# Bias and row maximum in one VectorE instruction, on negated logits, in two attention stages

## The reference

```python
q = rms_norm((h @ w_q).reshape(B, T, H, 2, d), q_norm)
s = jnp.einsum('bhcqd,bhckd->bhcqk', qb, k_sh) * scale          # scale = 64 ** -0.5 = 0.125
bias = -slopes[:, None, None] * dist                            # slopes = 2 ** -(h + 1)
s = jnp.where(dist >= 0, s + bias[None, :, None], -jnp.inf)
p = jax.nn.softmax(s, axis=-1)
attn = p[:, :, 0] - lam_full * p[:, :, 1]
o = jnp.einsum('bhqk,bhkd->bhqd', attn, v_sh)
```

```python
s_win = einsum(qr, k_win) * scale + bias
s_ctx = einsum(qr, kc) * scale
p = jax.nn.softmax(jnp.concatenate([s_win, s_ctx], axis=-1), axis=-1)
o = einsum(p_win, v_win) + einsum(p_ctx, vc)
```

## Time and profile before

| | |
|---|---|
| median of 3 runs | 3286.02 us (3283.83 to 3288.11) |
| the profiled execution | 3282.35 us |
| its span, first to last instruction | 3280.6 us |
| PE / DVE / ACT / POOL busy | 3061.7 / 1621.9 / 1126.9 / 134.8 us |
| mean granted TensorE clock | 0.962 |
| bytes moved | 234.75 MB, mean 72 GB/s |

### The profile page before, as it was taken

The page is one execution under the profiler, slowest core; times in us unless marked ns, Lnnn a source line. Parts: engine busy times, 40 slices in busy tenths (PEclk is TensorE's granted clock), DMA queues, the critical chain, the costliest instruction groups (busy, mean ns, idle before and its releaser), DMA issues.

```text
span 3280.6 us, 38579 instructions
## 1 busy us (share of the span) xinstructions
PE 3061.7 (93%) x15565; PEld 2389.7 (73%) x15565; DVE 1621.9 (49%) x2633; ACT 1126.9 (34%) x1821; POOL 134.8 (4%) x145
## 2 busy tenths in 40 slices
PE   7999898999999799999999999769999988987998
PEld 6888754666667688888788888547888865776886
DVE  5434454555555554344744345775435445336335
ACT  4322224444444333223332234453323243324332
POOL 0000001111211100000000000000000000101000
PEclk9999898999999899999999999879999988998999
DMA  4333212111110133333233332003333210201331
GB/s 125 96 99 97 83 61 67 41 41 41 42 29 21 44 105 97 97 97 92 82 97 98 99 98 95 1 1 103 98 95 92 80 54 1 78 23 52 94 90 58
DMA packets 186182, 234.75 MB, mean 72 GB/s; under 512 B 14201, under 2 KB 127446, under 8 KB 185750
## 3 DMA queue, kind: packets, MB, share of 16 engines
q1 hardware_dynamic: 186006, 232.29, 23.0%
HBM read 228.05 MB, written 4.19 MB: 71 GB/s over the span
## 4 chain that ended last, share of the span: by engine, by line
PE 86%; DVE 8%; ACT 3%; issue 2%; POOL 1%; DMA 0%; SPq 0%; DVEq 0%; ACTq 0%
PE banks L871 62%; PE banks L996 3%; PE banks L1028 2%; PE banks L982 1%; PE banks L1378 1%; PE banks L1369 1%; PE banks L1363 1%; PE banks L1019 1%; PE banks L1063 1%; PE banks L1092 1%; PE banks L1088 1%; PE banks L960 1%; DVE diff_scores L2391 1%; DVE diff_small L2397 1%; PE banks L1037 1%
## 5 line engine op out<-in xcount | busy, mean ns | idle before, releaser
L1935 DVE TENSOR_TENSOR weights_lo<-weights_raw,weights_hi 128x1024 fp32r<-128x1024 f32 (+3 forms) x377 | 453.4, 1206 | 996.9 <-ACT weights_hi L1454 996.3
L871 PE MATMUL banks<-operand_hi,weights_hi 128*128 128x512 f32 x2080 | 822.9, 396 | 34.8 <-DVE weights_lo L1935 13.1
L871 PE MATMUL banks<-operand_lo,weights_hi 128*128 128x512 f32 x2080 | 816.4, 392 | 0.0
L871 PE MATMUL banks<-operand_hi,weights_lo 128*128 128x512 f32 x2080 | 816.0, 392 | 0.0
L1454 ACT ACTIVATE weights_hi<-weights_raw 128x1024 fp32r<-128x1024 f32 (+3 forms) x377 | 391.9, 1043 | 1055.3 <-PE banks L871 1028.4
L871 PEld LDWEIGHTS banks<-operand_hi,weights_hi 128*128 128x128 f32 x2080 | 394.3, 190 | 125.7 <-issue 28.2
L871 PEld LDWEIGHTS banks<-operand_lo,weights_hi 128*128 128x128 f32 x2080 | 394.6, 190 | 83.2 <-issue 2.2
L871 PEld LDWEIGHTS banks<-operand_hi,weights_lo 128*128 128x128 f32 x2080 | 394.2, 190 | 83.5
L871 PE MATMUL banks<-hidden_ffn_hi,weights_hi 128*128 128x512 f32 x352 | 137.1, 390 | 0.0
L871 PE MATMUL banks<-hidden_ffn_lo,weights_hi 128*128 128x512 f32 x352 | 136.9, 389 | 0.0
L871 PE MATMUL banks<-hidden_ffn_hi,weights_lo 128*128 128x512 f32 x352 | 136.9, 389 | 0.0
(11 more groups left out here) (522 smaller groups left out, 4406.8 us busy)
## 6 DMA issues: line engine op xcount, KB each, us to landing
weights_raw<-in_ffn_w_in_dram SPq DMA_DIRECT2D x352, 256.0 KB, 3.2
weights_raw<-in_ffn_w_out_dram SPq DMA_DIRECT2D x88, 512.0 KB, 3.8
weights_raw<-in_w_in_dram SPq DMA_DIRECT2D x36, 512.0 KB, 3.7
weights_raw<-in_rwkv_w_rkv_dram SPq DMA_DIRECT2D x24, 512.0 KB, 4.3
weights_raw<-in_w_mod_dram SPq DMA_DIRECT2D x24, 512.0 KB, 5.5
weights_raw<-in_w_kv_dram SPq DMA_DIRECT2D x16, 512.0 KB, 3.7
weights_raw<-in_rwkv_w_o_dram SPq DMA_DIRECT2D x8, 512.0 KB, 5.6
weights_raw<-in_diff_w_q_dram SPq DMA_DIRECT2D x8, 512.0 KB, 4.9
```

Source lines behind the costliest of these rows:

```text
L871: mm = nc.tensor.matmul(o, l, r, start=first and t == 0 and job["opens"], stop=last and t == 2, **skip)
L1935: nc.vector.tensor_tensor(ring_lo[0:p, u["slot"], 0:n, 0:w], ring_raw[0:p, u["ring"], 0:n, 0:w], f32(ring_hi[0:p, u["slot"], 0:n, 0:w]), A ...
```

## The change

Logits are kept negated, so that the row's maximum becomes a minimum and can be used as the exponential's bias without a further step. One VectorE instruction, `tensor_tensor_reduce`, adds two tensors, multiplies by a constant, writes the result and also gives the minimum of the row (started from a scalar).

In the differential attention the slope of the head is divided out of the queries (`q_gain`, eight columns made at the start of the query stage), so that scores and distance can be added without a factor; the new instruction multiplies the sum by -0.125 times the slope. Maximum and negation of step 1 go, and ScalarE waits for step 0. In the neighbourhood attention the context keys are negated when they are copied; VectorE first reduces the minimum of the 256 context scores, then the new instruction adds the bias to the 512 window scores, negates, and continues that minimum. This all stands in step 0, lane by lane.

```diff
+            for h_ in range(DIFF_HEADS):
+                nc.vector.tensor_scalar(q_gain[:, h_:h_ + 1], vec("diff_q_norm"), 1.0 / slope(h_), None,
+                                        ALU.mult).then_inc(*dve_own.by())
...
-                        head_scale("q", ui - 1, q[:, ui - 1], vec("diff_q_norm"))
+                        if ui == 1:
+                            dve.wait_ge(*dve_own.now())
+                        head_scale("q", ui - 1, q[:, ui - 1], q_gain[:, ui - 1:ui])
...
                 if tb < TB and s == 0:
                     for c, b in ((0, A), (1, B)):
                         dve.wait_ge(*lane_pe[lane].at(("s", h_, tb, c)))
-                        nc.vector.scalar_tensor_tensor(
-                            out=S[:, lane, c, 0:n], in0=dist[:, (TB - 1 - tb) * P:T], scalar=8.0 * 2.0 ** (-(h_ + 1)),
-                            in1=ps[:, b, 0:n], op0=ALU.mult, op1=ALU.add).then_inc(*own.by(("bias", h_, tb, c)))
-                elif tb < TB and s == 1:
-                    for c in range(2):
-                        dve.wait_ge(*own.at(("bias", h_, tb, c)))
-                        nc.vector.tensor_reduce(sm[:, c:c + 1], S[:, lane, c, 0:n], AX_X, ALU.max).then_inc(*dve_own.by())
-                        dve.wait_ge(*dve_own.now())
-                        nc.vector.tensor_scalar(sm[:, 2 + c:3 + c], sm[:, c:c + 1], -0.125, None,
-                                                ALU.mult).then_inc(*own.by(("max", h_, tb, c)))
+
+                        nc.vector.tensor_tensor_reduce(
+                            out=S[:, lane, c, 0:n], in0=ps[:, b, 0:n], in1=dist[:, (TB - 1 - tb) * P:T],
+                            scale=-0.125 * slope(h_), scalar=3.0e38, op0=ALU.add, op1=ALU.min,
+                            accum_out=sm[:, 2 + c:3 + c]).then_inc(*own.by(("bias", h_, tb, c)))
...
-                        act.wait_ge(*lane_dve[lane].at(("max", h, tb, c)))
+                        act.wait_ge(*lane_dve[lane].at(("bias", h, tb, c)))
                         nc.scalar.activation(S[:, lane, c, 0:n], S[:, lane, c, 0:n], ACT.Exp, bias=sm[:, 2 + c:3 + c],
-                                             scale=0.125, accum_out=sm[:, 4 + c:5 + c]).then_inc(
+                                             scale=-1.0, accum_out=sm[:, 4 + c:5 + c]).then_inc(
...
                 nc.scalar.activation(kb[:, j["i"], at:at + w], ps[:, j["bank"], j["col"]:j["col"] + w],
-                                     ACT.Copy).then_inc(*evac_a.by(job))
+                                     ACT.Copy, scale=-1.0 if j["extra"] else 1.0).then_inc(*evac_a.by(job))
...
-                        nc.vector.tensor_tensor(ps[:, A], ps[:, A],
-                                                bias[:, lane, e0:e0 + NA_KR, :].rearrange("p e c -> p (e c)"),
-                                                ALU.add).then_inc(*own.by((name, "bias", hd, tb)))
-                    elif s == 1:
-                        if name == "na":
-                            dve.wait_ge(*own.at((name, "bias", hd, tb)))
-                        else:
-                            dve.wait_ge(*lane_pe[lane].at((name, "s", hd, tb)))
+
+                        nc.vector.tensor_reduce(sm[:, 0:1], ps[:, B, 0:CTX], AX_X, ALU.min).then_inc(*dve_own.by())
+                        dve.wait_ge(*dve_own.now())
+                        nc.vector.tensor_tensor_reduce(out=ps[:, A], in0=ps[:, A],
+                                                       in1=bias[:, lane, e0:e0 + NA_KR, :].rearrange("p e c -> p (e c)"),
+                                                       scale=-1.0, scalar=sm[:, 0:1], op0=ALU.add, op1=ALU.min,
+                                                       accum_out=sm[:, 1:2]).then_inc(*own.by((name, "bias", hd, tb)))
+                    elif s == 1 and name == "mla":
+                        dve.wait_ge(*lane_pe[lane].at((name, "s", hd, tb)))
```

More of the change, by code:

```diff
@@ L513, in program @@
                 for c in range(2):
-                    lane_dve[lane].expect(("max", h, tb, c))
                     lane_act[lane].expect(("exp", h, tb, c))
@@ L580, in attention_plan @@
                 elif s == 1:
-                    lane_dve[lane].expect((name, "max", hd, tb))
+                    if name == "mla":
+                        lane_dve[lane].expect((name, "max", hd, tb))
                     lane_act[lane].expect((name, "exp", hd, tb))
@@ L721, in program @@
                 subln = sb("subln", [P, 1], on=ph2)
+                q_gain = sb("q_gain", [P, DIFF_HEADS], on=ph2)
                 S = sb("diff_scores", [P, LANES, 2, T], on=ph2)
@@ L782, in mix_at, with slope @@
             return rkv[2][:, k] if n in ("a1", "v") else mixed[:, k % 4]
+        def slope(h):
+            return 8.0 * 2.0 ** (-(h + 1))
         class Lane:
@@ L1845, in attention @@
                     if s == 1:
-                        act.wait_ge(*lane_dve[lane].at((name, "max", hd, tb)))
+                        act.wait_ge(*lane_dve[lane].at((name, "max" if name == "mla" else "bias", hd, tb)))
                         nc.scalar.activation(probs_[:, lane], flat[:, 0:KEYS], ACT.Exp, bias=sm[:, 1:2], scale=scale,
@@ L1877, in act_program @@
             fence("qb")
-            attention("na", 1.0)
+            attention("na", -1.0)
             fence("na")
@@ L2371, in dve_program @@
                 dve.wait_ge(*dense_done.at(("job", job)))
-                nc.vector.scalar_tensor_tensor(out=q[:, t], in0=q[:, t], scalar=vec("diff_q_norm"),
+                nc.vector.scalar_tensor_tensor(out=q[:, t], in0=q[:, t], scalar=q_gain[:, t:t + 1],
                                                in1=ps[:, jobs[job]["bank"]], op0=ALU.mult,
```

## The result

The changed kernel takes 3238.19 us (median of 4 runs, 3237.07 to 3244.51), the kernel before, on the same chip, 3287.07 us (4 runs, 3283.83 to 3292.47). The ratio is 0.985, interval 0.9835 to 0.9872.

The account below looks back on a forecast made before the run. VectorE was taken to lead the differential attention, with TensorE 0.38 us behind, and late maxima to hold up the neighbourhood attention. Gains of 18.5 (neighbourhood) and 12 us (differential) off 3286.0 gave 3255.5 us, range 3240 to 3280.

Parts of the forecast that it names:

- Which stages, and what bounds each: Only the two attention stages gain; VectorE is the chain in the differential, ScalarE waits for maxima in the neighbourhood attention.
- The price of the new instruction: Both stages, on VectorE: costs what a plain addition does, 0.70 us at 512 columns, plus 0.10 for its result.
- (d): Both stages: new instruction at the scan's half rate, 1.24 us each at 512 columns; 3278 us, chance 0.15.
- (e): Both stages: new instruction has a fixed extra cost; at 1 us extra, 46 us lost, 3332 us, chance 0.10.
- The neighbourhood attention: Lane-by-lane step 0 without maxima and negations brings each group's end 2.3 us forward, eight groups: 18.5 us gained.
- (c): Both stages: TensorE's clock stays up once its stops are short; 40 us gained, 3246 us, chance 0.10.
- GpSimd's mask: Neighbourhood attention: masking the next heads' bias stays covered at the fourth lane, by 1.2 us.
- The differential attention: VectorE saves 1.4 to 1.5 us a round at 512 keys, TensorE takes most of it: 12 us gained.
- The terms: Differential attention, per set: start 0.5, 128 keys 1.5, 256 keys 0.4, 384 keys 2.4, 512 keys 1.5, end 1.5 us.
- The quarter off: Differential attention: 15.6 us for two sets cut to 12, as engines hand heads round and aren't always tight.
- (b): Differential attention bounded by TensorE throughout, only set ends and neighbourhood attention gain: 22.5 us, 3263 us, chance 0.15.
- The signs: Both stages: right if 512-key rounds take 3.8 us with TensorE in the chain; wrong if VectorE still leads them.

Follow-up runs that it names:

- the tails filled: The changed kernel with added 128x512 matmuls for nobody at the differential attention's start and in each head's tail, before the normalised-output wait: 3244.42 us, ratio 0.9862.

## Why the prediction was off

- **Which stages, and what bounds each.** Right. All that was gained lies in the two stages, and the two halves are independent (116.4 and 87.6 us alone).
- **The price of the new instruction.** Right: 0.70 us at 512 columns forecast, 0.684 and 0.759 measured. The rivals (d), half rate, and (e), a large fixed cost, are out by this row. The result, taken at 0.10 us, is 0.083 and 0.142 us as records; on the chain it is some 0.01 in the differential attention and 0.06 in the other. The rule that I had quoted from the Trainium skill (VectorE: DVE Perf Modes, Two Vector instructions with no wait between them), two instructions for an operation with an accumulator output, agrees with the trace: the second record is there for each.
- **The neighbourhood attention.** The mechanism was right and the size nearly: 18.5 us forecast, 21.1 measured. First transposes at +3.9, measured 2922.57 - 2918.69 = 3.88. ScalarE's waiting at some 35 us, measured 36.5. The missing part is the one that I had priced and left in rival (c): with the shorter stop the clock stays at 1.00 (0.87 before), so six transposes take 0.88 us, and the lanes end with VectorE's fourth. That gave 21 us, as measured. What was off here is the choice of 0.50 as the clock of the transposes after a shorter stop. That the shorter stop is what keeps the clock up was not tested by itself.
- **GpSimd's mask.** I had given it 1.2 us of cover. It has 0.2: the four masks end at 2945.2 us, and the fourth lane's step at the fifth group starts at 2945.45, as these lines of the timelines show. 0.44 us of the difference is a reading error of mine, for the wait stands ahead of the context minimum and not behind it; the rest is mostly the shorter group and the shorter lanes. The group is no longer for it (10.92 us). In the kernel with the tails filled the masks came later, and the fifth group took 11.68 us instead of 10.92.

```profile
2937.01 8.20 POOL L2689 TENSOR_TENSOR window_bias<-window_bias,window_mask 128x896 f32<-128x896 f32 x4 [115.72 <-DMA window_bias<-in_rpb_dram]
...
2945.45 0.42 DVE L2537 TENSOR_REDUCE attn_small<-banks 128x1 f32<-128x256 f32 x1
```

- **The differential attention.** Here the forecast fell short: 12 us, measured 28.8. VectorE's side of the sum was right: 1.4 to 1.5 us less per round at 512 keys forecast, 1.53 measured (4.01 to 2.48). The failed step is the sentence that TensorE's own work in that round is 3.83 us, so that it "stands 0.38 us behind VectorE, and becomes the bound at once". I took an observed stretch for a floor, and so kept 0.38 us of VectorE's 1.5. What the runs showed in its place: TensorE's floor in these rounds is 2.36 us, or 2.59 in the round that I had read at 3.83. VectorE's 2.48 leads them in the first set and stands 0.1 us from TensorE's in the second, so nearly all of its 1.53 us came through.
- **What had stretched the 3.83 us.** Two things. The first is the pair of maps, in which the second has to wait for ScalarE's copy, itself queued behind exponentials that were late because the maxima were. At 2110.92, at full clock, the maps run one after the other in 2.35 us; in the round that I had read, the second map's weights are loaded 0.94 us behind the first's, as the line below shows; after, the wait is over in time and the pair takes 1.13 to 1.23. Over the stage TensorE spends 34.6 us on scores instead of 50.7. The second is the clock: some 1.5 us of those 3.83 fell at 0.50 (the granted clock in each of the microseconds from 2119 to 2121; in the next it is 1.00 again), while after the change the first set's rounds at 384 and 512 keys run at 1.00 (2098.4 to 2122.2 us). Why it no longer falls there is argued from the shorter stops and not shown; over the whole stage the mean is 0.75 in both kernels.

```profile
2120.47 0.50 PEld L1269 LDWEIGHTS banks<-diff_keys,diff_queries 64*128 64x128 f32 x2 [0.44 <-ACT diff_out L1758]
```

- **The terms.** In the table above, the start came out smaller than forecast (1.2 for 2.0 us), 256 keys larger (1.7 for 0.4; the score matmuls there take 11.1 us over both sets instead of 14.5, at a granted clock of 0.50 in both kernels), 384 a little larger (3.1 for 2.4), and 512 keys with the end of the set three times as large (9.0 for 3.0). At 384 keys I had read TensorE's 0.76 us of standing as all there was to gain, which left out that the same wait held the maps apart.
- **The quarter off.** I took 3.6 us off for hand-overs. Nothing of the kind appeared, and without it the term would still have been 15.6, little more than half of what was measured.
- **Rivals.** (b), TensorE as the bound throughout (3263 us), is true of the second set, but at a level far below the one I gave it, and not of the first set's rounds at 384 and 512 keys. (c) was the nearest of all, 3246 us. It had the neighbourhood attention to the microsecond. In the differential attention its stretches at 0.50 did get shorter, from some 17 and 27 us at the starts of the two sets to 13.5 and 20.5 (2085 to 2098 and 2136 to 2156), but most of the gain lies in the rounds at 384 and 512 keys and at the sets' ends, outside of them. That its number came nearest is in part luck.
- **The signs.** Of those I had named as right, the instruction, the groups (10.92 for 11.2 us), the first transpose and ScalarE's waiting came out. The rounds of 3.8 us did not (2.25 to 2.78), though TensorE is in the chain of the second set; in the first set the rounds are still led by VectorE, which I had named as a sign of being wrong.
- **The range.** It ended at 3240 because (c) was its lower end and no case had TensorE's round itself shrinking. The bound I had written down, 68 us of TensorE's standing in both stages, would have allowed 48.9, but it was no bound, for the same reason: TensorE's busy time in the two stages fell too, from 100.5 to 84.5 and from 81.7 to 73.3 us. The Trainium skill (TensorE: Matmul & The Clock Gate, Part 3: Packing small matmuls — row/col tiling) says that matmuls in different row groups run at the same time, nearly for the price of one. The trace agrees where no wait comes between them: 2.35 us apart, 1.13 together. By the trace, a pair without that wait would have taken 1.2 us off the round that starts at 2110.92. In the round of the earlier trace rows it would have taken only some 0.4 (an estimate: the first map's records end at 2121.41 us, the second's at 2121.84); the rest of what lies between 3.83 and 2.59 is the clock.

## What to carry to other kernels

The time in which an engine works through its part of a round isn't its floor when the round is led by another engine: take out of it the waits between its instructions, the instructions that could overlap but for a late release, and the stretches at the lower clock, and only then compare. When work is taken from a leading engine, ask what the others do once their inputs come early; here TensorE became faster too. Reordering lanes for an early first result gained nothing here as long as the last lane was ready no sooner; look at when the last one is.

## What the runs showed of the hardware

- Two fp32 score matmuls of 64 rows and 512 columns in the two row halves take 1.13 us together and 2.35 one after the other, at a clock of 1.00. A one-column matmul of 128 rows between them keeps them apart (2.07 us each, at a clock of 0.50).
- With the pairs apart, TensorE's granted clock stayed at 0.50 (1.2 GHz) for 165 us in which it was busy for 152.8, two stretches of 68 us without a gap among them; with the same instruction ahead of the pair the clock came back to 1.00 (2.4 GHz) 17 us after it had fallen. What decides isn't settled here.
- Four matmuls of 128x512 in the 3.45 us in which TensorE stood at the start of the stage kept the clock at 1.00 for its first 38 us, where it had been 0.50 for 13. The run with the tails filled repeats this.
- The instruction that adds, scales, writes and reduces runs at the rate of the plain multiply-add on fp32 (0.684 us at 512 columns beside 0.678), plus a second record of 0.083 to 0.142 us for the minimum.
